# Low halves of the mix front's weights, units 2 to 4: a negated copy by ScalarE and adding transfers from GpSimd's queue in place of VectorE's subtractions

## The reference, cut to what matters

```
u = rmsnorm(h, mix_norm)
proj = u @ w_in          # [xp | q | k | v | gate_logits], 512 + 3*512 + 2*1024 columns
y_pool = pooling(xp) @ w_branch_pool
y_sb = stick_breaking_attention(q, k, v) @ w_branch_attn
h = h + (sigmoid(g_pool) * y_pool + sigmoid(g_sb) * y_sb) @ w_out
```

## Time and profile before

| | |
|---|---|
| runs | 1923.79, 1924.63, 1924.80 us |
| profiled execution, its own time | 1924.49 us |
| its span, first to last instruction | 1922.5 us |
| busy: TensorE, VectorE, ScalarE, GpSimd | 99%, 72%, 41%, 8% |
| granted TensorE clock, mean | 1.000 of full |
| transfers | 347 MB, all of a kernel's own from one hardware queue, 55.3% of 16 engines' span |

### The profile page before, as it was taken

The page is one execution under the profiler, slowest core; times in us unless marked ns, Lnnn a source line. Parts: engine busy times, 40 slices in busy tenths (PEclk is TensorE's granted clock), DMA queues, the critical chain, the costliest instruction groups (busy, mean ns, idle before and its releaser), DMA issues.

```text
span 1922.5 us, 25204 instructions
## 1 busy us (share of the span) xinstructions
PE 1911.0 (99%) x9046; PEld 1599.3 (83%) x9046; DVE 1392.9 (72%) x1714; ACT 786.7 (41%) x1170; POOL 152.1 (8%) x221
## 2 busy tenths in 40 slices
PE   9999999999999999999999999999999999999998
PEld 9888888888888888888888888898888888888886
DVE  6977867774566776786878878879777777755655
ACT  7423232323434543345665652464323232334344
POOL 1000000000000300002443420010000000000002
PEclk9999999999999999999999999999999999999999
DMA  5456654558676534248446347643545444677665
GB/s 165 147 198 228 225 174 149 189 196 312 210 236 196 185 110 151 73 134 236 142 127 175 105 154 254 191 136 114 182 141 197 148 168 153 220 265 240 204 195 200
DMA packets 246723, 347.19 MB, mean 181 GB/s; under 512 B 16368, under 2 KB 150256, under 8 KB 243056
## 3 DMA queue, kind: packets, MB, share of 16 engines
q1 hardware_dynamic: 246640, 346.10, 55.3%
HBM read 232.79 MB, written 112.98 MB: 180 GB/s over the span
## 4 chain that ended last, share of the span: by engine, by line
PE 95%; DVE 2%; DMA 1%; ACT 1%; issue 1%; POOL 1%; SPq 0%; POOLq 0%; DVEq 0%; ACTq 0%
PE bank L1233 39%; PE bank L1330 10%; PE bank L1277 8%; PE bank L1278 8%; PE bank L1279 8%; PE bank L1187 5%; PE bank L1471 4%; PE bank L1379 2%; PE bank L1407 2%; PE bank L1437 2%; PE bank L1543 2%; PE bank L1162 1%; PE bank L1562 1%; PE bank L1561 1%; PE bank L1528 1%; PE bank L1526 1%
## 5 line engine op out<-in xcount | busy, mean ns | idle before, releaser
L2171 DVE TENSOR_TENSOR dn_lo<-dn_lo_raw,dn_hi 128x1024 fp32r<-128x1024 f32 x149 | 181.9, 1223 | 150.9 <-ACT dn_hi L1741 150.5
L1233 PE MATMUL bank<-lo_t,wa_hi 128*128 128x512 f32 x640 | 249.0, 389 | 0.0
L1233 PE MATMUL bank<-hi_t,wa_hi 128*128 128x512 f32 x640 | 249.0, 389 | 0.0
L1233 PE MATMUL bank<-hi_t,wa_lo 128*128 128x512 f32 x640 | 249.0, 389 | 0.0
L1741 ACT ACTIVATE dn_hi<-dn_lo_raw 128x1024 fp32r<-128x1024 f32 x149 | 157.9, 1060 | 219.3 <-DMA dn_lo_raw<-act_dram 219.3
L1277 PE MATMUL bank<-dn_hi 128*128 128x512 f32 x596 | 232.5, 390 | 0.0
L1279 PE MATMUL bank<-dn_lo,dn_hi 128*128 128x512 f32 x596 | 231.9, 389 | 0.0
L1278 PE MATMUL bank<-dn_hi,dn_lo 128*128 128x512 f32 x596 | 231.9, 389 | 0.0
L1233 PE MATMUL bank<-hi_b,wa_hi 128*128 128x512 f32 x480 | 186.9, 389 | 0.9 <-DVE up L2295 0.9
L1233 PE MATMUL bank<-lo_b,wa_hi 128*128 128x512 f32 x480 | 186.8, 389 | 0.0
L1233 PE MATMUL bank<-hi_b,wa_lo 128*128 128x512 f32 x480 | 186.7, 389 | 0.0
(11 more groups left out here) (275 smaller groups left out, 3764.1 us busy)
## 6 DMA issues: line engine op xcount, KB each, us to landing
wa_lo_raw<-in_ffn_w_gate_up_dram SPq DMA_DIRECT2D x87, 512.0 KB, 4.9
dn_lo_raw<-act_dram SPq DMA_DIRECT2D x149, 256.0 KB, 4.3
act_dram<-g SPq DMA_DIRECT2D x44, 512.0 KB, 4.3
wd_t<-in_ffn_w_down_dram SPq DMA_DIRECT2D x44, 512.0 KB, 6.6
act_dram<-s_of SPq DMA_DIRECT2D x88, 256.0 KB, 6.4
wd_dram<-wd_t SPq DMA_DIRECT2D x22, 1024.0 KB, 5.9
dn_lo_raw<-wd_dram SPq DMA_DIRECT2D x85, 256.0 KB, 3.4
dn_lo_raw<-in_ffn_w_down_dram SPq DMA_DIRECT2D x64, 256.0 KB, 3.1
```

Of the source, the lines that this page charges most:

```text
L1233: last = nc.tensor.matmul(acc, lhs, rhs, start=n == 0 and i != 2 and i < 5, stop=n == 11, skip_group_check=True)
L2171: return nc.vector.tensor_tensor(dst, raw, hi.bitcast(f32), ALU.subtract)
```

## The change

For units 2 to 4, ScalarE writes the high half and, by a second activation with scale -1, the negated high half into `ws_lo`; the group's signal `mb_hi` comes after both. GpSimd's list gets 12 transfers (`mix_lo(b, g)`), each of which adds the raw group in `ws_raw` to `ws_lo`, so that the low half stands there; each waits for ScalarE's signal and for the one before to land (`mb_low_in`). They stand ahead of the memsets of `xpad`. VectorE's subtractions stay for unit 1 only. TensorE and SyncE wait for `mb_low_in` in place of `mb_lo` from unit 2 on (`mix_low_done`). The semaphores `wghi` and `wglo` become one, `wg_split`, and `mb_low_in` is new.

```
--- before.py
+++ after.py
@@ -458,13 +458,13 @@
         whi = sem("whi")
         wlo = sem("wlo")
         wpiece = sem("wpiece")
-        wghi = sem("wghi")
-        wglo = sem("wglo")
+        wg_split = sem("wg_split")
 
         mb_in = sem("mb_in")
         mb_sum = sem("mb_sum")
         mb_hi = sem("mb_hi")
         mb_lo = sem("mb_lo")
+        mb_low_in = sem("mb_low_in")
         mb_prod = sem("mb_prod")
         mb_copied = sem("mb_copied")
         mb_add = sem("mb_add")
@@ -639,6 +639,13 @@
         def mix_order(b, g):
 
             return 4 * b + (1, 3, 4, 2)[g]
+
+        def mix_low_done(engine, b, g=2):
+
+            if b:
+                engine.wait_ge(mb_low_in, 16 * (mix_order(b, g) - 4))
+            else:
+                engine.wait_ge(mb_lo, mix_order(b, g))
 
         def mix_free(engine, b, g):
 
@@ -876,7 +883,7 @@
             def load_values(half):
 
                 g = U_V[half]
-                sp_.wait_ge(mb_lo, 4 * NM)
+                mix_low_done(sp_, NM - 1)
                 for part in range(2):
                     k = 4 * half + 2 * part
                     sp_.dma_start(value_rows(w_raw, g % 2, 2 * part, 2), in_cols[:, k:k + 2, VC:VC + BR, :].rearrange(
@@ -886,7 +893,7 @@
 
                 kind, which = MIX_UNITS[b]
                 if b:
-                    sp_.wait_ge(mb_lo, 4 * b)
+                    mix_low_done(sp_, b - 1)
                 else:
                     sp_.wait_ge(whi, U_A[1] + 1)
                     sp_.wait_ge(wlo, U_A[1] + 1)
@@ -1386,7 +1393,7 @@
             def group_quad(m):
 
                 pe.wait_ge(ylo, 2 * m + 2)
-                pe.wait_ge(wglo, 1)
+                pe.wait_ge(wg_split, 2)
                 for b in range(4):
                     th, ab = b // 2, b % 2
                     if m:
@@ -1455,7 +1462,7 @@
                     if b >= 2 and i in (1, 3, 4):
                         pe.wait_ge(mb_add, 5 * (b - 2) + (1 if i == 1 else i + 1))
                     if i % 2 == 0:
-                        pe.wait_ge(mb_lo, mix_order(b, i // 2))
+                        mix_low_done(pe, b, i // 2)
                     if b == 0 and i in (2, 3, 4, 6):
                         pe.wait_ge(rt_lo, {2: 1, 3: 2, 4: 3, 6: 4}[i])
                     if i == 2:
@@ -1882,7 +1889,10 @@
                 else:
                     act.wait_ge(mb_sum, 4 * b + 2 * g)
                 mix_free(act, b, g)
-                nc.scalar.activation(ws_hi[:, mix_place(b, g)], ws_raw[:, mix_group(g)], ACT.Copy).then_inc(mb_hi, 1)
+                last = nc.scalar.activation(ws_hi[:, mix_place(b, g)], ws_raw[:, mix_group(g)], ACT.Copy)
+                if b:
+                    last = nc.scalar.activation(ws_lo[:, mix_place(b, g)], ws_raw[:, mix_group(g)], ACT.Copy, scale=-1.0)
+                last.then_inc(mb_hi, 1)
 
             def mix_first(b):
 
@@ -2026,7 +2036,7 @@
             pool_hi(0, 0)
             act.wait_ge(pool_in, 48)
             act.wait_ge(mb_add, 5 * NM)
-            nc.scalar.activation(wg_hi[:, :, :], wg_raw[:, :, :], ACT.Copy).then_inc(wghi, 1)
+            nc.scalar.activation(wg_hi[:, :, :], wg_raw[:, :, :], ACT.Copy).then_inc(wg_split, 1)
             pool_hi(0, 1)
             take_v(0)
             take_v(1)
@@ -2599,10 +2609,10 @@
                 dve.wait_ge(mb_sum, 4 * b + 2)
                 nc.vector.tensor_tensor(s4, a12, s2, ALU.subtract).then_inc(mb_sum, 1)
 
-            def mix_lo(b, g):
-
-                dve.wait_ge(mb_hi, mix_order(b, g))
-                low(flat(ws_lo[:, mix_place(b, g)]), flat(ws_raw[:, mix_group(g)]), flat(ws_hi[:, mix_place(b, g)])).then_inc(mb_lo, 1)
+            def mix_lo(g):
+
+                dve.wait_ge(mb_hi, mix_order(0, g))
+                low(flat(ws_lo[:, mix_place(0, g)]), flat(ws_raw[:, mix_group(g)]), flat(ws_hi[:, mix_place(0, g)])).then_inc(mb_lo, 1)
 
             def mix_c11(b):
 
@@ -2657,14 +2667,8 @@
                 if b + 1 < NM:
                     mix_weight_sums(b + 1)
                 mix_c22(b, 1)
-                if b + 1 < NM:
-                    mix_lo(b + 1, 0)
-                    mix_lo(b + 1, 3)
-                    mix_lo(b + 1, 1)
                 mix_out(b, 1, 1, 2)
                 mix_c12(b)
-                if b + 1 < NM:
-                    mix_lo(b + 1, 2)
                 mix_out(b, 0, 1, 3)
 
             chain = sem("chain")
@@ -2705,11 +2709,11 @@
 
             def group_weights_lo():
 
-                dve.wait_ge(wghi, 1)
+                dve.wait_ge(wg_split, 1)
                 nc.vector.tensor_tensor(wg_lo[:, :, :].rearrange("p g d -> p (g d)"),
                                         wg_raw[:, :, :].rearrange("p g d -> p (g d)"),
                                         wg_hi[:, :, :].rearrange("p g d -> p (g d)").bitcast(f32),
-                                        ALU.subtract).then_inc(wglo, 1)
+                                        ALU.subtract).then_inc(wg_split, 1)
 
             def pool_weight_sums(u):
 
@@ -2802,16 +2806,16 @@
             mix_weight_sums(0)
             mix_sums_lo(1, 2)
             mix_sums_lo(2, 0)
-            mix_lo(0, 0)
+            mix_lo(0)
             take_first(1, 0)
             mix_sums_lo(3, 3)
             take_first(1, 1)
             mix_sums_lo(4, 1)
             take_first(1, 2)
             take_first(1, 3)
-            mix_lo(0, 3)
-            mix_lo(0, 1)
-            mix_lo(0, 2)
+            mix_lo(3)
+            mix_lo(1)
+            mix_lo(2)
             for b in range(NM):
                 mix_unit(b)
             split(U_V[0] % 2, U_V[0] + 1, None)
@@ -3018,6 +3022,19 @@
                 pool.wait_ge(h_sp[t], 16)
             pool.wait_ge(xn_ok, 2 * NT)
             mix_raw(0)
+
+            def mix_lo(b, g):
+
+                pool.wait_ge(mb_hi, mix_order(b, g))
+                if mix_order(b, g) > 5:
+                    pool.wait_ge(mb_low_in, 16 * (mix_order(b, g) - 5))
+                dst, raw = ws_lo[:, mix_place(b, g)], ws_raw[:, mix_group(g)]
+                nc.gpsimd.dma_start(dst.rearrange("p s k f -> p (s k f)").bitcast(f32), raw.rearrange("p s k f -> p (s k f)"),
+                                    accum_op=ALU.add).then_inc(mb_low_in, 16)
+
+            for b in range(1, NM):
+                for g in (0, 3, 1, 2):
+                    mix_lo(b, g)
             for m in (1, 0):
                 xpad_free(pool, m, 1)
                 nc.gpsimd.memset(xpad[m][:, :, 0:PAD], 0.0).then_inc(const_set, 1)
```

6 lines of the change are left out of this document (removed).

## The result

The changed kernel takes 1946.24 us in the median of four runs (1945.47 to 1947.09) against 1924.51 of the kernel before, a ratio of 1.0113 with a 95% interval of 1.0100 to 1.0125: 21.7 us slower. The forecast was 1941.3, with a range of 1923.5 to 1966. The profiled execution took 1947.09 us with a span of 1945.3, 22.8 more than before. L1478 is now TensorE's line of the mix front (L1471 before), L1386 that of the values, L3032 GpSimd's transfers, L903 the weight loads, L908 the stores.

A forecast was written before the change was run, and what follows sets the result against it. TensorE was taken to bound the kernel, so relieving VectorE gains 0; the profiled 1924.49 us plus 16.8 (16.4 for the loop of load, activations and transfers, 0.4 for the value weights) gave 1941.3, range 1923.5 to 1966.

The forecast's parts named there:

- ScalarE's part: 12 more activations in units 2 to 4, 11.3 us, on an engine busy under half of this stage.
- d: Time of one adding 512 KB transfer on GpSimd's queue, taken as 5.0 us between bounds of 4.0 and 7.6.
- e: Time of one adding 256 KB transfer on GpSimd's queue, taken as 3.5 us between bounds of 2.6 and 5.9.
- The loop: Units 2 to 4: load 6.0, two activations 1.9, S; 26.4 us against TensorE's 19.04, making unit 4 end 16.4 us later.
- S: One unit's four chained transfers, three of d and one of e: 18.5 us.
- the value weights' load: After unit 4's last transfer: goes out at 791.4, lands 5.2 us later, and makes TensorE's third matmul there 0.4 us late.
- The displaced stores: Query and key tile stores behind the later loads: some 3 us each in units 2 and 3, inside the loop's lateness, nothing added.
- Hidden transfers: Rival, 17%: d under 3.3 us plus a little, so the transfers in units 2 to 4 cost nothing; 1924.5 us.
- Much slower transfers: Rival, 14%: adding has its own rate or displaced stores run beside the transfers; 1969 us, or 1950.9 with 5.9 and 4.3.
- The falling clock: Rival, 8%: TensorE's grant falls to 1.2 GHz after pauses in this stage; 2.7 to 5.4 us more, 1944 to 1947.
- Faster: Rival, 2%: without VectorE's reads the matmuls of units 2 to 4 step 15 ns faster; 3.9 us less, 1920.6 us.
- The signs that I named: Mix front: TensorE waits for transfers, loads at about 738.6 and 765, stretch 93 us; sixth-product waits alone would blame the stores.

The follow-up runs named there:

- e5: The kernel before with ScalarE's 12 added activations alone, VectorE's subtractions then writing the low halves as before: 1924.10 us.
- e6: The changed kernel with one semaphore per group, unchained transfers, and the next weights loaded once the transfers of groups 0 and 3 have landed: 1923.79 us.
- e1: The changed kernel with the stores of the query and key tiles ahead of the next unit's weight load in SyncE's queue: 1950.39 us.
- e9: The kernel before, with the weight loads of units 3 and 4 held until TensorE's fourth product of the unit in progress, no adding transfers: 1942.60 us.
- e3: The changed kernel with one semaphore per group, so that no transfer waits for the one before to land: 1928.88 us.
- e2: The changed kernel with the next unit's weights loaded once the transfers of groups 0 and 3 have landed: 1943.59 us.
- e8: The changed kernel with 26 more matmuls ahead of TensorE's wait at the sixth products of units 2 and 3: 1946.12 us.
- e11: The late-load kernel of e9 with 26 more matmuls ahead of the wait at the sixth products of units 2 and 3: 1939.50 us.

## Why the prediction was right

The sign, the size and the mechanism held; the time came out 4.9 us above the forecast, in the range. Point by point:

*What bounds the kernel.* As put: VectorE's relief gave nothing (e5 leaves it busy, e6 relieves it: 1924.1 and 1923.8).

*ScalarE's part:* cost nothing, e5.

*The transfers.* I had d = 5.0 and e = 3.5 from plain rows. Measured are 4.5 and 3.3 to landing plus 0.5 from a landing to the next start, which I had not listed: 5.0 and 3.8. That d fitted is thus in part luck: half a microsecond too much for the landing covered the gap that I had left out. In unit 2 the landings were forecast for 725.1, 728.6, 733.6 and 738.6, and came at 724.8, 728.7, 733.7 and 738.7.

*The loop.* The terms that were too small, by the chain of the profiled execution: S was 18.6, 20.2 and 19.1 us in the three units against 18.5 (2.4 in all; the first transfers of units 3 and 4 ran beside the displaced stores and took 5.0 and 5.2, and the second of unit 3 took 4.2); the loads 6.9 and 6.2 against 6.0 (1.1); the two activations with their waits 2.3 against 1.9 (0.8); the value weights' load 6.7 against 5.2 (1.5). That is 5.8, the distance of the profiled 1947.1 to 1941.3.

*The displaced stores.* "I add nothing" was right for the sum, since e1 shows that taking their wait away wins nothing. But I put their wait at some 3 us each and it was 6.6 and 6.5, and e9 shows that they were a path of 18.7 us by themselves, 3 us short of the loop. I had called it covered by the loop; it was a second bound, 0.4 to 0.6 us behind the first. To mend the stores alone wins nothing (e1), to take the transfers away and leave the load late wins 3 us (e9); what wins is to free the raw buffer early (e3, e6).

*The rivals.* Hidden transfers: refuted as the change stands; e6 is that case, made by undoing the chain and the load's lateness. Much slower transfers: refuted, 4.5 us. But beside loads and stores they take 7 to 10 (e1, e2), the condition that this rival named. (Of its two sums, 1950.9 has the 0.4 us of the value weights and 1969 leaves it out.) The falling clock: it did fall, as this rival had it, to 0.50 in both long pauses. Its price was hidden behind the loop (e8), where I had put 2.7 to 5.4 us on top; the one pause that mattered for it, before the last five products, was 0.4 us, and the grant stayed at 1.00 there. The Trainium skill's rule ("TensorE: Matmul & The Clock Gate", HAM oscillation), that waits for transfers between bursts can bring the lower level back, agrees with the granted clock of 0.50 here; TensorE's wait was for VectorE, and VectorE's for the stores. Faster: e6, where no wait is left in this stage, rules it out to 0.1%.

*The signs that I named.* The stretch of L1478 grew from 76 us to some 98 (93 forecast), the loads moved to 738.75 and 768.2 (738.6 and 765). Against the forecast, the largest waits were not at the transfers; I had written that waits at the sixth product alone would make the stores the price. They weren't alone, but nearly, and e1 shows that reading it so would have been wrong. The waits for transfers that I had put at the starts and third products of units 3 and 4 came at the third products only, 0.6 and 0.4 us, because the waits at the sixth products had come first.

## What to carry to other kernels

A step that is moved to a slower way can be free, as in e6, if its end holds nothing back that is due: look at what its end releases (here the single raw buffer, and behind the load the stores of a ring), and add up that loop, not the step. In a chain of short transfers nothing moved for about half of the time: a semaphore for each brought back 17 of 21.7 us, and loading each slot when its own reader is done brought back the rest. Where the waits name one engine and the chain another, take it as two paths that are late, and test each with the other in place.

## What the runs showed of the hardware that I had not expected

- A transfer from GpSimd's queue, SBUF to SBUF, 512 KB, lands in 4.5 us with adding and 2.9 without, 256 KB in 3.3 and 2.3; issuing takes GpSimd 0.87 us with adding and 0.54 without. Two or three adding ones at a time land in 4.8 to 5.9 us each on otherwise quiet queues (e3). The transfer engines are full (share 0.98) for 2.8 us of an adding 512 KB transfer and for about 1.3 us of a plain one, and idle before and after.
- Beside 1 MB of loads and 2 MB of stores from SyncE's queue the same adding transfer takes 9.1 to 9.7 us (e2).
- TensorE's granted clock fell to 0.50 within pauses of 6.6 us and was back at 1.00 some 3 to 5 us after the work went on. For two pauses the fall cost between nothing that can be told from zero (e8) and 3 to 4 us (e11), by what else was late.
